# Residual additions on VectorE, four first tiles chunk by chunk, and late highs and lows spread over the down tiles, in a two-block transformer kernel

## Chip, cores and metric

One core of a Trainium2 chip runs one launch. The metric is the device time in microseconds, the median of repeated executions.

## The reference

The first block has two layers; the second adds gated deltanet, differential attention and a routed mixture of experts. The change lies in the first block and at the seam to the second. Cut to what matters:

```python
def rms_norm(x, gain):
    return x * rsqrt(mean(x * x, -1) + EPS) * gain

def hybrid_layer(x, ...):                       # twice
    h = rms_norm(x, attn_pre_gain)              # norm 1
    ...                                         # h @ w_in, two attentions, gates
    x = x + rms_norm(mixed @ w_out, attn_post_gain)          # norm 2
    h = rms_norm(x, ffn_pre_gain)                            # norm 3
    x = x + rms_norm(conv_ffn(h, w_up, conv, w_down), ffn_post_gain)   # norm 4
    return x
```

512 tokens, 1024 channels, 2816 hidden channels in each half of w_up, all float32. Behind the second layer the deltanet's input projection reads x directly.

## The kernel before

Activations lie channels by tokens: 8 chunks of 128 channels by 512 tokens. A float32 product is made of three rounded ones: each operand is split into a high part (a rounded copy, made by ScalarE) and a low part (the difference, made by VectorE), and `product` (L729 to L733) issues high × high (L731), high weight × low activation (L732) and low weight × high activation (L733). A tile of outputs (128 channels) is 8 chunks of such products, 24 matmuls, and reads one slot of weights.

**Weights.** SyncE streams 512 KB slots into a ring of 8 (L509), each as soon as the tile eight slots back has been used. ScalarE casts a slot to its high part into one of two buffers `highs` (`cast_weights`, L1420), which it may only do when the tile two before has been used; VectorE then splits off the low part in place in the ring (`split_weights`, L2035). Each engine works its list in program order, so a cast or a split that waits holds back all behind it. In layer 0 `fm` are the first tiles, then compression, token-major, gate, branch, `out`, 44 `up` and 22 `down` tiles.

**Norms.** Squares are made by ScalarE, added up by VectorE into `total`, and summed over the partitions by a matmul with ones (L788 to L798); ScalarE makes the reciprocal root `rs` (L1460, L1463). Norms 1 and 3 scale behind the products: their tiles are multiplied by `rs` when VectorE evicts them (L2165 in fm, L2296 in up), so the products can begin before `rs` is there. Norms 2 and 4 scale first: `residual_and_lows` (L2058) lets VectorE make the scaled chunk (L2063), GpSimd adds it to x (L582, function `added`), ScalarE makes the high of the sum (L1453, L1690) and its square (L1455), and VectorE the low (L2055, L2343), three chunks behind the scaling. While this runs, TensorE does a few products that nobody reads (`idle_products`, L766).

**First tiles behind a norm.** `first_pair` goes through two tiles at once, chunk by chunk: it waits for the low of chunk k, then issues the 6 products of that chunk. Its two weight highs lie in `first_high`, a part of tmp. Tiles 2 and on follow one by one (`tile`, L735); the norm's sum goes in front of tile 3; tile r uses PSUM bank r % 4 and waits, from tile 4 on, for the eviction of tile r − 4.

**Up and down.** Per up tile VectorE evicts (L2296), does a three-tap convolution (L2306, L2310), splits one coming slot, and once in two tiles multiplies (`finish`, L2285). The eviction of tile r + 1 stands in front of the convolution of tile r. ScalarE does the casts and gelu (L1614). For the down tiles the 22 chunks of the result are split into highs (`high_g`, L1619) and lows (`low_g`, L2290): 7 of them during up, 8 in one block behind it (the highs ahead of the cast of the third down tile, the lows ahead of its split), the rest one per down tile. Down tile 0 needs the eviction of the last up tile before it touches bank 0.

**Other places.** `cmp` products of the two compression blocks (L836) use banks 1 and 2 and wait for the evictions of fm tiles 9 and 10. The deltanet tiles use L1714 for eviction on ScalarE and a four-tap convolution on VectorE (L2431, L2434); behind their first pair come the a/b products (L1014), and then small decay terms (L1698 to L1703, L2391).

## Time and profile before

| | us |
|---|---|
| median of 3 runs | 3549.63 (3541.72 to 3550.85) |
| the profiled execution, its span | 3550.9 |

```profile
span 3550.9 us, 50016 instructions
## 1 busy us (share of the span) xinstructions
PE 3408.3 (96%) x16710; PEld 2674.1 (75%) x16710; DVE 2485.3 (70%) x3707; ACT 1888.2 (53%) x2964; POOL 379.1 (11%) x371
```

These are busy time, share of the span and number of instructions of each engine: PE is TensorE's matmuls, PEld its weight loads, DVE VectorE, ACT ScalarE, POOL GpSimd, SP SyncE. A busy TensorE is not one at its peak: the clock that it was granted, and matmuls that nobody reads, are not seen in this share. The chain of work that ended last, by engine:

```profile
PE 87%; DVE 6%; ACT 3%; issue 2%; DMA 1%; POOL 0%; ACTq 0%; SPq 0%; POOLq 0%; DVEq 0%
```

A timeline row is start, duration, engine, line, instruction, what it writes and reads, and in brackets the idle time of its engine before it and what ended that. Rows with a count merge instructions that follow each other, and their duration is that of all of them. Durations of single rows overlap: the next instruction of an engine starts a little before the last one's recorded end.

### The profile page before, as it was taken

How to read it: one execution, taken by the hardware profiler on the slowest of the kernel's cores; microseconds unless marked ns; L12 is line 12 of the kernel's file. 1: busy time of each engine (PE TensorE's matmuls, PEld its weight loads, DVE VectorE, ACT ScalarE, POOL GpSimd, SP SyncE). 2: the span in 40 equal slices, each digit the busy share in tenths (PEclk: the TensorE clock that was granted, in tenths of full speed). 3: DMA queues.
4: the chain of work that ended last, by engine and by line, in shares of the span. 5: the costliest groups of instructions: out<-in, count | busy, mean ns of one | idle time of the engine just before them, and what ended most of it. 6: DMA issues, size and time to landing. Idle time of an engine off the chain costs nothing.

```text
span 3550.9 us, 50016 instructions
## 1 busy us (share of the span) xinstructions
PE 3408.3 (96%) x16710; PEld 2674.1 (75%) x16710; DVE 2485.3 (70%) x3707; ACT 1888.2 (53%) x2964; POOL 379.1 (11%) x371
## 2 busy tenths in 40 slices
PE   8999999999999999999989998999999999999997
PEld 6766788787766788787778876888888676778885
DVE  6676577727677577726656547999999556579996
ACT  5666422325566422324542335888888446268885
POOL 0010100001010100001034201111111000011110
PEclk9999999999999999999999998999999999899999
DMA  4211232232211222222200007999999321189995
GB/s 163 78 43 51 75 101 95 89 100 77 78 43 54 77 95 95 92 97 86 83 30 1 7 18 260 358 364 368 358 372 386 122 72 35 42 296 371 388 382 199
DMA packets 161082, 541.88 MB, mean 153 GB/s; under 512 B 28192, under 2 KB 28192, under 8 KB 160800
## 3 DMA queue, kind: packets, MB, share of 16 engines
q1 hardware_dynamic: 141408, 510.37, 40.0%
q0 software_dynamic: 16256, 16.84, 1.4%
q10 hardware_dynamic: 3264, 12.58, 0.9%
q8 instruction: 100, 1.64, 0.2%
q14 instruction: 54, 0.44, 0.0%
HBM read 547.02 MB, written 34.60 MB: 164 GB/s over the span
## 4 chain that ended last, share of the span: by engine, by line
PE 87%; DVE 6%; ACT 3%; issue 2%; DMA 1%; POOL 0%; ACTq 0%; SPq 0%; POOLq 0%; DVEq 0%
PE psum L731 24%; PE psum L733 23%; PE psum L732 23%; PE psum L1031 4%; PE psum L881 2%; PE psum L913 2%; PE psum L895 1%; PE psum L1222 1%; DVE arena L2063 1%; PE psum L805 1%; PE psum L1228 1%; DMA arena<-rows_out_m 1%; PE psum L1171 1%; DVE arena L2391 1%; ACT highs L1420 1%
## 5 line engine op out<-in xcount | busy, mean ns | idle before, releaser
L2742 DVE TENSOR_TENSOR ew_r<-arena,ehigh_r 128x1024 fp32r<-128x1024 f32 x648 | 750.5, 1219 | 25.6 <-ACT ehigh_r L1887 25.2
L1420 ACT ACTIVATE highs<-ring 128x1024 fp32r<-128x1024 f32 x292 | 308.4, 1057 | 683.7 <-PE psum L733 677.9
L1887 ACT ACTIVATE ehigh_r<-arena 128x1024 fp32r<-128x1024 f32 x648 | 632.3, 1053 | 37.1 <-DVE arena L2733 24.0
L2035 DVE TENSOR_TENSOR ring_rounded<-ring,highs 128x1024 fp32r<-128x1024 f32 x292 | 358.4, 1228 | 417.6 <-ACT highs L1420 417.5
L733 PE MATMUL psum<-oab_r,ring_rounded 128*128 128x512 f32 x1424 | 563.8, 396 | 0.0
L731 PE MATMUL psum<-oab_r,highs 128*128 128x512 f32 x1360 | 558.6, 411 | 5.1 <-DVE fm_r L2255 4.3
L732 PE MATMUL psum<-h_r,highs 128*128 128x512 f32 x1232 | 484.3, 393 | 0.0
L731 PE MATMUL psum<-ehigh_r,xT_high_r 128*128 128x512 f32 x864 | 352.9, 408 | 12.9 <-issue 6.6
L733 PE MATMUL psum<-ehigh_r,xT_low_r 128*128 128x512 f32 x864 | 341.2, 395 | 0.0
L732 PE MATMUL psum<-ew_r,xT_high_r 128*128 128x512 f32 x864 | 339.6, 393 | 0.0
L731 PEld LDWEIGHTS psum<-oab_r,highs 128*128 128x128 f32 x1360 | 256.2, 188 | 92.1 <-issue 33.4
L733 PEld LDWEIGHTS psum<-oab_r,ring_rounded 128*128 128x128 f32 x1424 | 268.8, 189 | 59.0
L732 PEld LDWEIGHTS psum<-h_r,highs 128*128 128x128 f32 x1232 | 232.1, 188 | 44.4 <-issue 1.0
L731 PEld LDWEIGHTS psum<-ehigh_r,xT_high_r 128*128 128x128 f32 x864 | 164.3, 190 | 45.9 <-issue 15.3
L733 PEld LDWEIGHTS psum<-ehigh_r,xT_low_r 128*128 128x128 f32 x864 | 163.9, 190 | 38.5
L732 PEld LDWEIGHTS psum<-ew_r,xT_high_r 128*128 128x128 f32 x864 | 164.6, 191 | 31.9
L731 PE MATMUL psum<-ehigh_r,hT_high_r 128*128 128x512 f32 x432 | 170.4, 394 | 4.4 <-DVE hT_low_r L2755 4.4
L1031 PE MATMUL psum<-arena 128*128 128x128 f32 x1216 | 156.4, 279 | 14.8 <-issue 5.1
L733 PE MATMUL psum<-ehigh_r,hT_low_r 128*128 128x512 f32 x432 | 169.3, 392 | 0.0
L1031 PEld LDWEIGHTS psum<-arena 128*128 128x128 f32 x1216 | 146.8, 193 | 28.9 <-issue 16.8
L732 PE MATMUL psum<-ew_r,hT_high_r 128*128 128x512 f32 x432 | 167.6, 388 | 0.0
L582 POOL TENSOR_TENSOR x<-x,arena 128x512 f32<-128x512 f32 x32 | 52.6, 1670 | 938.4 <-DVE arena L2063 938.4
(383 smaller groups left out, 6249.4 us busy)
## 6 DMA issues: line engine op xcount, KB each, us to landing
arena<-in_moe_w SPq DMA_DIRECT2D x648, 512.0 KB, 5.9
ring<-in_wstream SPq DMA_DIRECT2D x312, 512.0 KB, 3.4
arena<-rows_out_m ACTq DMA_DIRECT2D x8, 1024.0 KB, 8.1
rows_in_m<-arena ACTq DMA_DIRECT2D x4, 1024.0 KB, 4.0
x<-in_xT SPq DMA_DIRECT2D x8, 256.0 KB, 7.2
result<-x SPq DMA_DIRECT2D x8, 256.0 KB, 2.1
const<-in_const SPq DMA_DIRECT2D x1, 1112.5 KB, 9.6
arena<-rows_in_m,arena POOLq DMA_INDIRECT x58, 6.4
```

Of the source, the lines that this page charges most:

```text
L582: pool.tensor_tensor(x[:, k, :], x[:, k, :], src[:, k, :], ALU.add) \
L731: pe.matmul(acc, lhs[0], rhs[0], start=start, stop=False)
L732: pe.matmul(acc, lhs[0], rhs[1], start=False, stop=False)
L733: return pe.matmul(acc, lhs[1], rhs[0], start=False, stop=stop)
L805: mm = pe.matmul(psum[:, bank, :], ones, src[:, k, :], start=(i == 0), stop=(i == KD - 1))
L881: pe.matmul(psum[:, 2 * (p % 2) + g, 0:width(p)], q[:, qt * P:(qt + 1) * P], keys, start=True, stop=True).then_inc(pe_done, seq.step(f"h{p ...
L913: mm = pe.matmul(acc, values[:, KEYS[kind], kts[i], dims], ptbuf[:, u, i * P:(i + 1) * P], start=first and i == 0, stop=last and i == n - 1)
L1031: mm = pe.matmul(psum[:, bank, c], lhsT[:, c], rhs[:, c], start=True, stop=True)
L1420: act.activation(highs[:, r % HIGHS, :], ring[:, r, :], ACT.Copy) \
L1887: act.activation(ehigh_r[p], ew[:, p, :], ACT.Copy).then_inc(expert_cast[mi], 1)
L2035: dve.tensor_tensor(ring_r[:, c % R, :], ring[:, c % R, :], high.bitcast(F32), ALU.subtract).then_inc(weights_split, seq.step(ch="split"))
L2742: TT(ew_r[p], ew[:, p, :], ehigh_r[p].bitcast(F32), ALU.subtract).then_inc(expert_split[mi], 1)
```

## The change

- GpSimd's `added` is gone. `residual_and_lows` adds each chunk to x on VectorE, right behind its scaling (and behind the low of two chunks before); norm 4's chunks 0 to 3 are first copied out of PSUM.
- `first_four` replaces `first_pair` behind norm 4 and norm 2 (fm of layer 1, up, deltanet); layer 0's first stage keeps `first_pair`. It goes through four tiles chunk by chunk: behind the high of chunk k come 8 products, behind its low 4 more. Four weight highs lie in tmp and in fm or siga. ScalarE and VectorE cast and split four tiles and a fifth ahead of the norm's scaling.
- Tile 4 gets a bank of its own and holds the norm's sum matmul in its middle. From tile 5 on the banks go (r − 5) % 4, and tile r waits for the eviction of the tile that had its bank. In fm the column products of `rs` come behind tile 4.
- In up, fm of layer 1 and deltanet the split of tile 5 stands before the stage, and the first split within it, that of tile 6, behind the work on tile 2 (deltanet: 4).
- The sums of norms 2 and 4 take one more square through VectorE and one fewer through TensorE; there are fewer idle products.
- The last up tile is evicted ahead of the split behind the convolution of tile 41. The 15 late highs and lows are spread: two behind each of the first four down tiles' casts and splits, then one each.
- The compression blocks wait for fm tiles 10 and 11.

```diff
+        LATE_HIGHS = {k: [] for k in range(PAIRS)}
+        for n in range(EARLY, PAIRS):
+            LATE_HIGHS[(n - EARLY) // 2 if n < EARLY + 8 else n - EARLY - 4].append(n)
+        first_high = two_highs("first_high", tmp[:, 0:4])
+        up_high = first_high + two_highs("up_high", fm[:, 0:4])
+        next_high = first_high + two_highs("next_high", siga[:, 4:8])
+        def bank_of_tile(r):
+            return r if r < 5 else (r - 5) % 4
-                    added("n2", y)
-                    added("n4", h)
...
+            def scaled_tile(stage, r, between=None):
+                if r >= 5:
+                    pe.wait_ge(dve_done, seq.at(f"{stage}.d{bank_before(r)}"))
+                w = [v.rearrange("p (k c) -> p k c", c=P) for v in weights()]
+                for k in range(KD):
+                    if k == KD // 2 and between:
+                        between()
+                    mm = product(psum[:, bank_of_tile(r), :], [v[:, k, :] for v in w], both_parts(k), k == 0, k == KD - 1)
+                mm.then_inc(slot_used, seq.step(f"{stage}.t{r}", ch="slot"))
+            def first_four(lows, stage, parts, high):
...
+                for k in range(KD):
+                    x_high, x_low = parts(k)
+                    pe.wait_ge(act_done, seq.at(f"{lows}.hi{k}"))
+                    for i in range(4):
+                        pe.matmul(psum[:, i, :], w[i][0][:, k, :], x_high, start=(k == 0), stop=False)
+                        pe.matmul(psum[:, i, :], w[i][1][:, k, :], x_high, start=False, stop=False)
+                    pe.wait_ge(dve_done, seq.at(f"{lows}.lo{k}"))
+                    for i in range(4):
+                        mm = pe.matmul(psum[:, i, :], w[i][0][:, k, :], x_low, start=False, stop=(k == KD - 1))
...
+                    first_four("n1", "fm", both_parts, next_high)
+                    scaled_tile("fm", 4, lambda: added_sums("n1", total))
...
-                    pe.wait_ge(dve_done, seq.at(f"fm.d{9 + kv}"))
+                    pe.wait_ge(dve_done, seq.at(f"fm.d{10 + kv}"))
...
-                sums_in_parts("n2", total, oab8, (6, 7))
-                idle_products(7, 5)
-                first_pair("n3", "up", both_parts)
+                sums_in_parts("n2", total, oab8, (7,))
+                idle_products(3, 5)
+                first_four("n3", "up", both_parts, up_high)
+                scaled_tile("up", 4, lambda: added_sums("n3", total))
...
-                sums_in_parts("n4", total, sq, (4, 5, 6))
+                sums_in_parts("n4", total, sq, (5, 6))
-                idle_products(4, 7)
+                idle_products(3, 7)
...
-            first_pair("xdn", "dn", lambda k: [xh[:, k, :], xl[k]])
+            first_four("xdn", "dn", lambda k: [xh[:, k, :], xl[k]], next_high)
...
-                for k in range(EARLY, EARLY + 8):
-                    high_g(k)
                 for k in range(PAIRS):
                     if k + HIGHS < PAIRS:
                         cast_weights()
+                    for n in LATE_HIGHS[k]:
+                        if n >= EARLY + 8:
+                            act.wait_ge(slot_used, seq.at(f"down.t{n - EARLY - 8}"))
+                        high_g(n)
...
-                first_weights()
-                cast_weights(2 + passed)
+                first_weights(next_high)
+                cast_weights(4 + passed)
                 for c in (7, 0, 1, 2, 3, 4, 5, 6):
...
-                for k in range(KD + 3):
+                for k in range(KD + 2):
                     if k < KD:
                         dve.scalar_tensor_tensor(dst[:, k, :], src(k), gain[:, k:k + 1], rs, ALU.mult, ALU.mult) \
                             .then_inc(dve_done, seq.step(f"{stage}.t{k}"))
-                    if k >= 3:
-                        low_k(k - 3)
+                    if k >= 2:
+                        low_k(k - 2)
+                    if k < KD:
+                        dve.wait_ge(dve_done, seq.at(f"{stage}.t{k}"))
+                        dve.tensor_tensor(x[:, k, :], x[:, k, :], dst[:, k, :], ALU.add) \
+                            .then_inc(dve_done, seq.step(f"{stage}.x{k}"))
...
-                    if 1 <= r <= NFM - 3:
+                    if (1 if l == 0 else 2) <= r <= NFM - 3:
                         split_weights(1)
...
-                    if r + 1 < 2 * PAIRS:
+                    if r + 1 < 2 * PAIRS - 1:
                         up_out(r + 1)
...
-                    if 1 <= r <= 2 * PAIRS - 3:
+                    if r == 2 * PAIRS - 3:
+                        up_out(2 * PAIRS - 1)
+                    if 2 <= r <= 2 * PAIRS - 3:
                         split_weights(1)
...
-                split_weights(2, of=first_high)
+                split_weights(4, of=next_high)
+                split_weights(1)
                 dve.wait_ge(pe_done, seq.at("down.c7"))
                 dve.tensor_copy(h[:, 7, :], psum[:, 7, :]).then_inc(dve_done, seq.step("down.d7"))
-                sum_of_squares("n4", sq, (7, 0, 1, 2, 3))
+                sum_of_squares("n4", sq, (7, 0, 1, 2, 3, 4))
+                for c in range(4):
+                    dve.tensor_copy(h[:, c, :], psum[:, c, :]).then_inc(dve_done, seq.step(f"down.d{c}"))
```

## Rows read from the trace of the kernel before

**Rows 1.** TensorE waits, whole span: us in total, times, longest us.
```profile
PE psum L731 <- DVE h_r L2055: 25.9, 13, 13.8
...
PE psum L731 <- DVE ring_rounded L2035: 5.3, 2, 2.7
...
PE psum L731 <- DVE arena L2296: 1.8, 2, 0.9
```

**Rows 2.** Timeline, norm 2, layer 0: start us, us, instruction, [idle before].
```profile
422.82 4.76 DVE L2063 SCALAR_TENSOR_TENSOR arena<-arena,small 128x512 f32<-128x512 f32 x4 [5.05 <-ACT arena L1463]
...
429.41 0.47 PE L731 MATMUL psum<-oab_r,first_high 128*128 128x512 f32 x1 [1.99 <-DVE h_r L2055]
...
431.54 1.76 DVE L2063 SCALAR_TENSOR_TENSOR arena<-arena,small 128x512 f32<-128x512 f32 x1
...
450.25 1.02 PE L798 MATMUL psum<-arena,const 128*128 128x512 f32 x2
...
452.02 0.63 ACT L1463 ACTIVATE arena<-arena 128x512 f32<-128x512 f32 x1
```

**Rows 3.** Timeline, VectorE: chained additions; lows; scalings read from PSUM (layer 0).
```profile
443.54 4.67 DVE L2078 TENSOR_TENSOR arena<-arena 128x512 f32<-128x512 f32 x6
...
686.46 4.90 DVE L2290 TENSOR_TENSOR g_r<-arena,oab_r 128x512 fp32r<-128x512 f32 x8
...
811.05 2.73 DVE L2063 SCALAR_TENSOR_TENSOR arena<-psum,small,arena 128x512 f32<-128x512 f32 x4 [4.62 <-ACT arena L1463]
```

**Rows 4.** Timeline, VectorE in the up tiles of layer 0.
```profile
454.77 1.28 DVE L2296 TENSOR_TENSOR arena<-psum,arena 128x512 f32<-128x512 f32 x2
...
464.40 1.22 DVE L2035 TENSOR_TENSOR ring_rounded<-ring,highs 128x1024 fp32r<-128x1024 f32 x1
```

**Rows 5.** Windows around the start of the down tiles, layers 0 and 1.
```profile
core 0: us, PE busy (x) PEld busy (x) DVE busy (x) ACT busy (x) POOL busy (x), PEclk, DMA share, GB/s
680.00:700.00 20.00, 16.44 (x58) 12.58 (x57) 14.68 (x23) 9.13 (x14) 0.00 (x0) 0.83 0.19 61
1480.00:1500.00 20.00, 16.44 (x71) 12.79 (x70) 16.11 (x24) 10.71 (x16) 0.00 (x0) 1.00 0.23 79
```

**Rows 6.** Timeline, norm 1 to fm in layer 1, TensorE, VectorE and ScalarE.
```profile
815.08 0.47 PE L731 MATMUL psum<-oab_r,first_high 128*128 128x512 f32 x1 [0.97 <-DVE h_r L2055]
...
839.51 0.68 DVE L2165 TENSOR_TENSOR arena<-psum,arena 128x512 f32<-128x512 f32 x1
...
847.02 0.69 DVE L2165 TENSOR_TENSOR arena<-psum,arena 128x512 f32<-128x512 f32 x1
...
848.35 1.06 ACT L1420 ACTIVATE highs<-ring 128x1024 fp32r<-128x1024 f32 x1 [5.53 <-PE psum L733]
...
853.87 1.06 ACT L1420 ACTIVATE highs<-ring 128x1024 fp32r<-128x1024 f32 x1 [1.84 <-PE psum L733]
```

**Rows 7.** Timeline, end of the down tiles of layer 1.
```profile
1601.05 1.06 ACT L1420 ACTIVATE highs<-ring 128x1024 fp32r<-128x1024 f32 x1 [2.56 <-PE psum L733]
...
1601.68 0.69 DVE L2333 COPY arena<-psum 128x512 f32<-128x512 f32 x1 [1.56 <-PE psum L733]
```

**Rows 8.** SyncE's ring loads from 1590 to 1630 us.
```profile
DMA to landing us min/median/max: 3.2/3.4/4.0
```

**Rows 9.** Timeline, first deltanet tiles.
```profile
1629.72 9.79 PE L1014 MATMUL psum<-small,x 128*128 128x16 f32 x64
...
1644.91 0.18 DVE L2391 TENSOR_SCALAR arena<-arena 128x32 f32<-128x32 f32 x1
...
1648.65 2.33 DVE L2434 SCALAR_TENSOR_TENSOR arena<-arena,small 128x512 f32<-128x512 f32 x3
...
1664.58 0.60 ACT L1714 ACTIVATE arena<-psum 128x512 f32<-128x512 f32 x1 [3.95 <-PE psum L733]
```

**Rows 10.** Timeline, compression products and the evictions of the last fm tiles, layer 0.
```profile
90.44 7.25 PE L836 MATMUL psum<-arena,ring 128*128 128x62 f32 x64
...
94.98 0.69 DVE L2165 TENSOR_TENSOR arena<-psum,arena 128x512 f32<-128x512 f32 x1
```

More of the change, by code:

```diff
@@ L576, in _ @@
             seq.note("zeroed")
-            def added(stage, src):
-                for k in range(KD):
-                    pool.wait_ge(dve_done, seq.at(f"{stage}.t{k}"))
-                    pool.tensor_tensor(x[:, k, :], x[:, k, :], src[:, k, :], ALU.add) \
-                        .then_inc(pool_done, seq.step(f"{stage}.x{k}"))
             for l in range(LAYERS):
@@ L789, in sums_in_parts @@
                 pe.wait_ge(dve_done, seq.at(f"{stage}.acc"))
-                pe.matmul(psum[:, bank, :], ones, acc, start=False, stop=False)
+                pe.matmul(psum[:, bank, :], ones, acc, start=(len(apart) == 1), stop=False)
                 pe.wait_ge(act_done, seq.at(f"{stage}.sq{apart[-1]}"))
@@ L1016, in _ @@
             mm.then_inc(pe_done, seq.step("ab.t"))
-            for n in range(2, 24):
+            for n in range(4, 24):
                 for k in range(KD):
@@ L2321, in _ @@
                 seq.note("down.g")
-                for k in range(EARLY, EARLY + 8):
-                    low_g(k)
                 for k in range(PAIRS):
```

112 lines of the change are left out of this document (65 added, 47 removed).

## Prediction, made before the changed kernel was run

> **What bounds the kernel now.** The page's header and its chain of waits come first: TensorE is busy for most of the span and the chain runs through its products, so time is only to be had where TensorE has nothing to do or works slowly. Next the waits of TensorE: by far the largest is that of the first products behind a norm for the low halves h_r, 25.9 us over 13 waits; the two places where a down tile waits for its split weights cost 5.3, and those where it waits for the last eviction of the up stage, 1.8 [rows 1]. These are the three things the change touches. Last, the timelines at the four norms show what makes a chunk late. In norm 2 the scaled chunks start at 422.82, the first product at 429.41, almost 7 us later [rows 2]. The scaling is four instructions in 4.76, and one later takes 1.76 beside a GpSimd addition; the same instruction fed from PSUM needs 2.73 for four [rows 2, 3]. A chunk's way is scaling, GpSimd addition, high, low; with 1.76 for the scaling and 0.6 for the low VectorE gives one in 2.4 us, while two tiles can use one in 6 × 0.23 = 1.38.
>
> A product is 0.23 us: a tile of 24 takes 853.87 − 848.35 = 5.52 [rows 6]. A signal from a tile's last product comes some 0.3 behind the time at which TensorE could issue the next.
>
> The Trainium skill (SBUF — State Buffer, Who interferes with whom) says that a VectorE instruction with two SBUF inputs and a GpSimd one that reads SBUF exclude each other for their whole length. By that rule the slow 1.76 goes when the additions leave GpSimd; the trace agrees, and its rows alone carry the prices below.
>
> **Norm 2 to up, both layers.** Removed: GpSimd's 8 additions, one sum matmul ahead of the reciprocal root (L798's kind, 1.02, of which I take 0.85), some idle products, which nothing waits for. Added on VectorE: per chunk one addition. Prices on VectorE alone: a chained addition 4.67/6 = 0.78, a low 4.90/8 = 0.61, a scaling 0.68 [rows 3]. One chunk is then 0.7 + 0.7 + 0.6 = 2.0 us, under the 4 × 3 × 0.23 = 2.76 that four tiles use. So TensorE paces the stretch, with no wait inside it.
>
> Start of scaling: 422.82 − 0.85 = 422.0. First high: scaling 0.74, addition 0.78, a ScalarE pass of 0.63 (L1463, same shape [rows 2]), 0.15 for signals: first product at 424.3 instead of 429.41. It needs only the high; the low of chunk 0 comes about 0.1 after the eight high products, taken as 0.1. Four tiles end at 424.3 + 22.1 + 0.1 = 446.5. Tile 4 holds the sum matmul in its middle (449.3) and ends, with 0.6 for it, at 452.6. From the sum matmul to rs it is 452.02 + 0.63 − 450.25 = 2.4 [rows 2], so rs stands at 451.7 and tile 0 is evicted at 452.4: tile 5 starts on time and ends at 458.2.
>
> Then the new wait. Tile 6 needs its split, which VectorE now issues only after the conv of tile 2, since the split of tile 5 has been moved ahead. Before, from the first eviction to the end of the split behind conv 3 tiles on it was 464.40 + 1.22 − 454.77 = 10.85 [rows 4], with one split (1.15) in between that is gone: 9.7. Ready at 451.7 + 9.7 = 461.4, a stall of 3.2 us. (ScalarE isn't later: its cast follows the end of tile 4 and one gelu.) Before, tile 6 started at 450.25 + 0.6 + 3 × 5.52 = 467.4. Net gain 6.0 per layer, **12.0** in all; bounds per layer are 9.2 (no stall) and 4.5 (a chunk at the 2.76 edge, first product 1.5 later). Splits after that are due at most every 5 us and the stall is not repeated.
>
> **Clock.** The windows of the down starts have the same TensorE work and the same 2.65 us stall in them, and the clock falls to its lower level in the one (0.83 over 20 us, 3.4 us of full-rate time lost) and not in the other (1.00) [rows 5]. The new stall of 3.2 is longer, so I expect the lower of the two levels (1.2 against 2.4 GHz) behind it more often than not: 0 to 3.4 per layer, 2.4 taken: **−4.8**.
>
> **Down start, both layers.** The last up tile is evicted ahead of a split, not behind it, so the 0.9 goes. Eight highs and eight lows in a block stood ahead of the cast and split of down tile 2; now that cast follows tile 0, two highs and lows follow it, and the others go two, then one, behind each next tile. Tile 2's split waits only for the last two finishes (about 1 us before TensorE needs it), tile 3's is done 2 to 3 us early. Highs 7 to 14 are needed five tiles (27 us) later; they are hidden. Gain 5.3 + 1.8 = **7.1** [rows 1], and the clock fall of layer 0, **3.2** (bounds 0 to 3.4) [rows 5]. If the cover fails it is a split and two lows, 2.4, per layer.
>
> **Norm 4 to fm, layer 1.** ScalarE now casts five tiles, and VectorE splits four and one, ahead of the copy of bank 7 that starts the squares. The fifth cast waits for the end of down tile 20, as the cast at 1601.05 does in layer 1; cast 1.06 and split 1.22 put the copy of layer 1 at 1603.3 instead of 1601.68 [rows 4, 7], and that of layer 0 1.6 later likewise. One sum matmul less takes 0.85 off and one more addition puts some back: scaling starts about 1.3 later. The way to the first product was 815.08 − 811.05 = 4.0 [rows 3, 6] and is 2.3: first product at 814.7. Four tiles to 836.9, tile 4 with its sum to 843.0, the four column products about 1.2, tile 5 to 849.7. rs is at 836.9 + 2.76 + 2.4 = 842.1. The split of tile 6 follows two evictions with their blocks, a third eviction and itself: 847.02 − 839.51 − 1.25 + 0.6 + 1.2 = 8.1 [rows 6], ready at 850.2, a stall of 0.5. Before, tile 6 started at 853.6. Gain **3.4**. Layer 0's first stage is fed by loads as before; its evictions only change banks: 0.
>
> **Norm 4 to deltanet.** Here the fifth cast is also queued behind a transfer. Ring slots are refilled eight tiles on, and with the two padding slots the fifth tile's slot is the one that down tile 20 frees, at about 1601. It lands 3.4 later [rows 8], so ScalarE's squares and VectorE's copy, both queued behind that cast and split, wait too: copy at 1601.1 + 3.4 + 1.1 + 1.2 = 1606.9, 5.2 later than 1601.68, scaling 4.5 later, first product 4.5 − 1.7 = 2.8 later. TensorE has no work for over 5 us there. The pair before ended at 1629.5. How long it took is read in layer 1's fm, worked back from tile 4's signal through three tiles, the sum and the columns: 848.35 − 0.3 − 3 × 5.52 − 0.6 − 1.2 − 815.08 = 14.6 [rows 6]. So the four end at 1629.5 − 14.6 + 2.8 + 22.2 = 1639.9. The a/b products follow; from them to the end of VectorE's decay terms it is 15.4 [rows 9], then convs 2, 3 and 4 (2.33 + 0.47 each) and the split of tile 6: 25.1 behind the four, 1665.0. Before, tile 6 started at 1664.3. Loss 0.7, in which 1.3 is a stall for that split; the clock's fall in the empty stretch costs 1 to 4, 2.5 taken: **−3.2**. Bound the other way: the slot is there in time, +2.3.
>
> **Compression.** Its second block of products now waits for tile 11's eviction, 94.98 + 0.69 = 95.7, and could have begun at 90.44 + 7.25/2 = 94.1 [rows 10]. Behind it a wait for ScalarE takes some of that: 0 to 1.6 per layer, 0.9 taken, **−1.8**.
>
> **Sum.** 12.0 − 4.8 + 7.1 + 3.2 + 3.4 − 3.2 − 1.8 = 15.9 us. Off the profiled 3550.9 this is 3535.0; the median of the runs, 3549.6, is 1.3 lower, which gives 3533.7, **3534**.
>
> **Rivals.**
> The stalls are hidden: the clock stays up behind them and the slot arrives in time. 4.8 + 2.5 + some of the 6.5 of stalls back: about 3525. For it: layer 1's 2.65 without a fall; against: the longer pause.
> The clock falls more: at every pause of 2 us or more, norm 4 of layer 0 among them, and for the full length. 1.0 more at each tile 6, 2 at norm 4, 1.5 at deltanet, 2 to 3 on the way: 3543. For it: the rows at the lower level; against: the pauses at norm 4 are broken by sum matmuls.
> The change doesn't do what it says: the five casts and splits delay the scaling in norm 2 as in norm 4, 4 us per layer: 3542. Against: there they begin two tiles before the end of the out stage.
> Slower: VectorE's two-input scalings and lows keep the 1.76 with GpSimd idle. A chunk is 1.76 + 1.76 + 0.78 = 4.3, 1.5 over 2.76; over 8 chunks and 4 norms 49 us less the 15.9: about 3582. It decides from a chunk of 3.25 on (15.9/32 over 2.76). Against: 0.61 for a low [rows 3].
> The chunk is slow for another reason: VectorE pauses behind every instruction. With a pause of half an instruction's length a chunk is 1.5 × (0.74 + 0.74 + 0.69) = 3.3, 0.5 over: 17 us, 3551. The eight lows in 4.90 leave no such gap [rows 3]. The Trainium skill (VectorE: DVE Perf Modes, The DRAIN you can't avoid) has such a pause as a rule, the instruction's length less 266 ns; by it a chunk would be about 3.5 and the time, an estimate, 3555; the trace does not bear it out here.
>
> **Chances.** Forecast 0.54, hidden stalls 0.18, more clock falls 0.18, late casts 0.05, slow VectorE 0.03, pauses 0.02. The forecast's own range is 3528 to 3541. The range of 8 in 10 takes in the first rivals' centres: 3524 to 3544. A measurement of this kernel tells 0.3% (10.7 us, 3539) from no change. Faster: 0.18 and nine tenths of 0.54, 0.67. Slower 0.03, same 0.30.
>
> **What would show it.** Right: no wait for h_r over 0.5 us inside the four tiles; about 22 us from first high product to their end; a wait for ring_rounded of some 3.2 at tile 6 of up in each layer and 0.5 at fm; no wait for ring_rounded at down tile 2; an empty TensorE of over 5 us at the end of layer 1 behind a cast that waits for a load. Wrong: chunks arriving slower than 2.76, a low over 0.8, or a stall at a down tile further on.

## The result, and the profile after

| | before | after |
|---|---|---|
| median | 3546.83 us (3540.22 to 3553.04, 20 runs) | 3540.10 us (3534.15 to 3542.81, 20 runs) |
| the profiled execution, its span | 3550.9 | 3532.3 |

The ratio is 0.9981, with a 95% interval of 0.9974 to 0.9987: the change gains 6.7 us, a small gain, but the interval leaves out no change at all. The forecast was a gain of 15.9 and a time of 3534; the time lies in the range of 3524 to 3544, but the gain is under half of what was forecast and within the 0.3% that was called no change, to which 0.30 was given, where 0.67 was given to faster.

The two profiled executions differ by 18.6 us, far more than the medians do. The one of after is the fastest of its 20. The part behind 1713.63 us of before, in which no line is changed, took 3550.9 − 1713.63 = 1837.3 us, and 3532.3 − 1702.99 = 1829.3 in after, with a granted clock of 0.98 against 0.97. These 8.0 us are no gain of the change, and the comparison by stages below stops ahead of them.

The page of after, in its header:

```profile
## 1 busy us (share of the span) xinstructions
PE 3392.3 (96%) x16682; PEld 2669.3 (76%) x16682; DVE 2488.3 (70%) x3751; ACT 1887.1 (53%) x2964; POOL 326.6 (9%) x339
```

GpSimd has lost its 32 additions and VectorE has gained them. VectorE's busy time is hardly more, since its scalings no longer run beside GpSimd. The waits of TensorE in the first 1760 us of after (us in total, times, longest):

```profile
PE psum L737 <- DVE h_r L2098: 13.0, 1, 13.0
PE psum L737 <- DVE ring_rounded L2078: 9.4, 4, 3.2
PE psum L825 <- ACT arena L1694: 5.8, 2, 4.4
...
PE psum L877 <- DVE arena L2213: 3.2, 2, 1.6
```

Of the 13 waits for h_r [rows 1] the first of the program is left. The waits for ring_rounded now stand elsewhere than in before: two at tile 6 of up, one at tile 6 of the deltanet and a small one at fm. The wait of L825 (the first sum matmul of norm 4, for the squares) and that of L877 (the second block of the compression, for the eviction of tile 11) are new. The last evictions of up, waited for at L731 in before, are not among them.

**Norm 2.** VectorE, ScalarE and TensorE behind the reciprocal root of layer 0, where before had [rows 2]:

```profile
425.00 0.75 DVE L2106 SCALAR_TENSOR_TENSOR arena<-arena,small 128x512 f32<-128x512 f32 x1 [3.16 <-ACT arena L1503]
425.78 0.69 DVE L2112 TENSOR_TENSOR x<-x,arena 128x512 f32<-128x512 f32 x1
...
426.51 0.72 ACT L1493 ACTIVATE oab_r<-x,small 128x512 fp32r<-128x512 f32 x1 [0.60 <-DVE x L2112]
...
427.37 0.47 PE L777 MATMUL psum<-oab_r,first_high 128*128 128x512 f32 x1 [1.22 <-ACT oab_r L1493]
...
429.70 0.74 DVE L2106 SCALAR_TENSOR_TENSOR arena<-arena,small 128x512 f32<-128x512 f32 x1
430.37 0.74 DVE L2098 SCALAR_TENSOR_TENSOR h_r<-x,small,oab_r 128x512 fp32r<-128x512 f32 x1
431.03 0.68 DVE L2112 TENSOR_TENSOR x<-x,arena 128x512 f32<-128x512 f32 x1
431.63 0.74 DVE L2106 SCALAR_TENSOR_TENSOR arena<-arena,small 128x512 f32<-128x512 f32 x1
...
463.53 1.22 DVE L2078 TENSOR_TENSOR ring_rounded<-ring,highs 128x1024 fp32r<-128x1024 f32 x1
...
464.89 0.47 PE L737 MATMUL psum<-oab_r,highs 128*128 128x512 f32 x1 [2.98 <-DVE ring_rounded L2078]
```

The first product comes 2.4 us behind the first scaling, where before needed 6.6 [rows 2], and a chunk takes 431.63 − 429.70 = 1.93 on VectorE. Tile 6 waits 2.98 for its split.

**By stages.** The scalings behind the norms and the first products of the compression are good marks. Those of before that are not in the rows ahead of the prediction are these, and the last is a deltanet tile behind which nothing differs:

```profile
892.26 1.00 PE L836 MATMUL psum<-arena,ring 128*128 128x62 f32 x8
...
1225.95 1.42 DVE L2063 SCALAR_TENSOR_TENSOR arena<-arena,small 128x512 f32<-128x512 f32 x2 [5.06 <-ACT arena L1463]
...
1611.32 1.41 DVE L2063 SCALAR_TENSOR_TENSOR arena<-psum,small,arena 128x512 f32<-128x512 f32 x2 [4.62 <-ACT arena L1463]
...
1713.63 0.47 PE L731 MATMUL psum<-x_part,highs 128*128 128x512 f32 x1 [1.07 <-ACT arena L1714]
```

and those of after:

```profile
89.37 3.68 PE L877 MATMUL psum<-arena,ring 128*128 128x62 f32 x32
...
804.34 0.75 DVE L2106 SCALAR_TENSOR_TENSOR arena<-arena,small 128x512 f32<-128x512 f32 x1 [1.13 <-ACT arena L1503]
...
881.47 1.22 PE L877 MATMUL psum<-arena,ring 128*128 128x62 f32 x10
...
1217.23 0.75 DVE L2106 SCALAR_TENSOR_TENSOR arena<-arena,small 128x512 f32<-128x512 f32 x1 [3.18 <-ACT arena L1503]
...
1600.73 0.75 DVE L2106 SCALAR_TENSOR_TENSOR arena<-arena,small 128x512 f32<-128x512 f32 x1 [2.28 <-ACT arena L1503]
...
1702.99 0.47 PE L737 MATMUL psum<-x_part,highs 128*128 128x512 f32 x1 [1.08 <-ACT arena L1757]
```

The forecast column puts the terms of the prediction into the stage where they fall (norm 2 to up: 0.85 of the 6.0 ahead of the scaling, 5.15 behind it; the late scalings of norm 4, 1.3 and 4.5, behind the down tiles).

| stage (us) | before | after | change | forecast |
|---|---|---|---|---|
| start to compression, layer 0 | 90.44 [rows 10] | 89.37 | −1.1 | 0 |
| to the scaling of norm 2, layer 0 [rows 2] | 332.4 | 335.6 | +3.2 | +0.05 |
| to the scaling of norm 4, layer 0 [rows 3] | 388.2 | 379.3 | −8.9 | −8.2 |
| to the compression, layer 1 | 81.2 | 77.1 | −4.1 | −4.7 |
| to norm 2, layer 1 | 333.7 | 335.8 | +2.1 | +0.05 |
| to norm 4, layer 1 | 385.4 | 383.5 | −1.9 | −1.8 |
| to the deltanet tile | 102.3 | 102.3 | −0.05 | −1.3 |
| sum | 1713.6 | 1703.0 | −10.7 | −15.9 |

Five of the seven come within about 1.3 us of their forecast. The two that don't are the stretches with the compression: 3.2 and 2.0 us too slow, 5.2 together, which is all of the difference between 15.9 and 10.7.

**Compression.** The timeline of its products in after, layer 0 (before: 64 products in 7.25 [rows 10]):

```profile
94.65 5.36 PE L877 MATMUL psum<-arena,ring 128*128 128x62 f32 x32 [1.61 <-DVE arena L2213]
...
100.26 0.54 PE L738 MATMUL psum<-ring_rounded,oab_r 128*128 128x408 f32 x1
100.60 0.54 PE L739 MATMUL psum<-highs,h_r 128*128 128x408 f32 x1
```

The wait of 1.6 us is the one that was predicted. What was not predicted is behind it: the second 32 products take 5.36 us where the first took 3.68, and the products behind it have a pitch of 0.34, where at the full clock it is 0.18 to 0.19 (shown with the idle products below). That is the lower level of the clock (1.2 GHz), and the windows of the two kernels say so (columns as in [rows 5]):

```profile
80.00:100.00 20.00, 18.39 (x107) 16.51 (x106) 15.71 (x23) 14.47 (x23) 0.00 (x0) 0.91 0.46 154
100.00:120.00 20.00, 20.00 (x106) 19.10 (x106) 7.48 (x16) 8.32 (x19) 0.00 (x0) 0.91 0.32 106
```

These two rows are from after. In before the window of 100 to 120 us has 1.00, and so has this one:

```profile
80.00:100.00 20.00, 20.00 (x125) 18.04 (x124) 15.66 (x22) 14.49 (x22) 0.00 (x0) 1.00 0.51 163
```

Twice 0.09 of 20 us is 3.6 us of full-rate time lost (the same work would have taken that much less at the higher level). This gave the theory for the experiments: **the change does what was forecast, and the compression's short wait, by the clock that falls behind it, takes back most of what is missing.** The rivals: the norms part never gained what the rows suggested; the other new waits (tile 6, norm 4) carry the miss; the gain of the down start is smaller than forecast.

### The profile page after: what moved, and what is told of

It is laid out like the page before. It is cut to its first block, busy times and chain, and to the rows that moved or that the text cites. A ratio compares the mean times of both kernels' runs of the same rounds, so it can differ in the third digit from the quotient of the medians.

```text
span 3532.3 us, 49964 instructions
## 1 busy us (share of the span) xinstructions
PE 3392.3 (96%) x16682; PEld 2669.3 (76%) x16682; DVE 2488.3 (70%) x3751; ACT 1887.1 (53%) x2964; POOL 326.6 (9%) x339
## 4 chain that ended last, share of the span: by engine, by line
PE 88%; DVE 5%; ACT 4%; issue 1%; DMA 1%; POOL 0%; ACTq 0%; SPq 0%; POOLq 0%; DVEq 0%
PE psum L737 23%; PE psum L739 22%; PE psum L738 22%; PE psum L1071 4%; PE psum L922 2%; PE psum L954 2%; PE psum L936 1%; PE psum L1262 1%; PE psum L777 1%; PE psum L778 1%; PE psum L781 1%; PE psum L842 1%; DVE ring_rounded L2078 1%; PE psum L1268 1%; DMA arena<-rows_out_m 1%
## 5 line engine op out<-in xcount | busy, mean ns | idle before, releaser
L1460 ACT ACTIVATE highs<-ring 128x1024 fp32r<-128x1024 f32 x284 | 300.1, 1057 | 650.1 <-PE psum L739 640.3
L2078 DVE TENSOR_TENSOR ring_rounded<-ring,highs 128x1024 fp32r<-128x1024 f32 x284 | 348.8, 1228 | 398.4 <-ACT highs L1460 398.3
L737 PE MATMUL psum<-oab_r,highs 128*128 128x512 f32 x1312 | 540.7, 412 | 11.3 <-DVE ring_rounded L2078 6.2
L739 PE MATMUL psum<-oab_r,ring_rounded 128*128 128x512 f32 x1328 | 526.7, 397 | 0.0
L738 PE MATMUL psum<-h_r,highs 128*128 128x512 f32 x1184 | 467.1, 395 | 0.0
L737 PEld LDWEIGHTS psum<-oab_r,highs 128*128 128x128 f32 x1312 | 247.7, 189 | 97.4 <-issue 40.9
L739 PEld LDWEIGHTS psum<-oab_r,ring_rounded 128*128 128x128 f32 x1328 | 251.3, 189 | 55.0
L738 PEld LDWEIGHTS psum<-h_r,highs 128*128 128x128 f32 x1184 | 224.0, 189 | 42.2 <-issue 1.0
L597 POOL TENSOR_TENSOR arena<-arena 128x512 f32<-128x512 f32 x32 | 40.9, 1279 | 1076.9 <-ACT arena L1610 1076.9
```

The lines of the kernel that those rows point to most:

```text
L597: pool.tensor_tensor(big[:, n * T:(n + 1) * T], big[:, n * T:(n + 1) * T], rs, ALU.mult) \
L737: pe.matmul(acc, lhs[0], rhs[0], start=start, stop=False)
L738: pe.matmul(acc, lhs[0], rhs[1], start=False, stop=False)
L739: return pe.matmul(acc, lhs[1], rhs[0], start=False, stop=stop)
L1460: act.activation(highs[:, r % HIGHS, :], ring[:, r, :], ACT.Copy) \
L2078: dve.tensor_tensor(ring_r[:, c % R, :], ring[:, c % R, :], high.bitcast(F32), ALU.subtract).then_inc(weights_split, seq.step(ch="split"))
```

## Experiments

All are measured in the same way as the pair above, beside runs of the kernel before on the same chip, which had medians of 3548.3, 3547.0 and 3548.4 in the three groups of runs. Differences below are worked out from the ratios (0.001 is 3.5 us), and an interval of a ratio is 2 to 5 us to either side, so that of a difference of two kernels 4 to 7. The kernel after was not run again in these groups; it is compared through before, whose medians lie within 1.6 us of each other. Each kernel was profiled once, and its stages are read from that one execution.

| kernel | median | ratio to before | to after |
|---|---|---|---|
| after | 3540.1 | 0.9981 (0.9974 to 0.9987) | |
| down part alone | 3533.5 | 0.9959 (0.9946 to 0.9972) | −7.8 |
| norms part alone | 3550.9 | 1.0007 (0.9998 to 1.0016) | +9.2 |
| norms part, no wait in the compression | 3542.5 | 0.9982 (0.9973 to 0.9991) | +0.4 |
| after, no wait in the compression | 3528.7 | 0.9948 (0.9933 to 0.9963) | −11.7 |
| after, idle products over that wait | 3533.7 | 0.9971 (0.9960 to 0.9982) | −3.5 |
| after, all up splits earlier | 3548.4 | 1.0003 (0.9992 to 1.0014) | +7.8 |
| after, only tile 6's split earlier | 3530.8 | 0.9957 (0.9943 to 0.9970) | −8.5 |
| after, fifth cast behind the squares | 3531.8 | 0.9954 (0.9940 to 0.9969) | −9.6 |
| after, additions on GpSimd again | 3548.1 | 1.0006 (0.9996 to 1.0016) | +8.9 |
| all mends together | 3517.5 | 0.9921 (0.9908 to 0.9935) | −21.3 |

**The two parts by themselves.** The kernel before, with the changes at the start of the down tiles and nothing else:

```
+        LATE_HIGHS = {k: [] for k in range(PAIRS)}
...
+                    if r == 2 * PAIRS - 3:
+                        up_out(2 * PAIRS - 1)
                     if 1 <= r <= 2 * PAIRS - 3:
                         split_weights(1)
...
                     if k + HIGHS < PAIRS:
                         split_weights(1)
-                    if k + EARLY + 8 < PAIRS:
-                        low_g(k + EARLY + 8)
+                    for n in LATE_HIGHS[k]:
+                        low_g(n)
```

> The kernel before with one part of the change alone: the late highs and lows spread over the down tiles and the last up tile evicted ahead of a split; the norms, the additions on GpSimd and the first pairs stay. Forecast's step: the two waits at the down start, 2.65 and 0.9 in each layer, are gone, 7.1 us, and the clock fall behind the longer one, which only some executions have, 0 to 6.8 more: 7 to 11 us under the kernel before. Rival A (the down start carries the whole measured gain, the norms give nothing): the same 7, and then the whole change is no better than this. Rival B (the spread highs and lows make a later down tile wait): under 3 us gained, and a wait for ring_rounded or a low further on in the down tiles.

It is 3533.5 us, 14.5 under before by the ratio, with 10.3 forecast for this part (7.1 and 3.2). The forecast is inside the interval of 10 to 19, at its small end. By the profiled executions, from the scaling of norm 2 to that of norm 4, it is 381.1 us in both layers against 388.2 and 385.4 in before: 7.1 and 4.3, together 11.3. Unlike in the profiled execution of before, this kernel has no stretch at the lower clock between 350 and 900 us. The complement, the changed kernel with these edits taken back:

> The change without its down-projection part: the norms (residual additions on VectorE, first four tiles chunk by chunk, split and cast places, the freed slots) as in the kernel after, the late highs and lows and the last eviction at the start of the down projection as in the kernel before. The down part alone had the ratio 0.9959, and the whole change 0.9981, so by subtraction the norms part alone should lose about 8 us: my theory gives 1.0010 to 1.0035. The rival, that parts do not add because the down part's gain is luck of the clock, gives 0.998 here as well. The forecast's own sum for this part, 12.0 + 3.4 - 3.2 - 4.8 - 1.8 = 5.6 us of gain, would be 0.9984.

The norms part alone is 2.5 us slower than before (0.7 faster to 5.7 slower; 3.5 to 12 slower was expected), where its terms in the forecast sum to a gain of 5.6. The parts add up to a gain of 12 and the whole gains 6.7; with intervals of this size the difference is not told from none. So the miss of the prediction lies in the norms part, about 8 us of it.

**The compression without its wait.** In after, the blocks use banks 1 and 2, of which bank 2 is freed last but one; here they use banks 0 and 1, each free in time.

```
-                    pe.wait_ge(dve_done, seq.at(f"fm.d{10 + kv}"))
+                    pe.wait_ge(dve_done, seq.at(f"fm.d{9 + kv}"))
...
-                            mm = pe.matmul(psum[:, 1 + kv, 0:2 * NC], w[:, i, :],
+                            mm = pe.matmul(psum[:, kv, 0:2 * NC], w[:, i, :],
...
                     pe.wait_ge(act_done, seq.at("cmp.hid1"))
+                    pe.wait_ge(dve_done, seq.at("fm.d11"))
```

> The changed kernel, but the compression blocks collect in banks 0 and 1 and wait for fm tiles 9 and 10, as before the change, and not for tile 11. Theory W (the 1.6 us wait in the middle of the small products also brings the clock down, which costs as much again): 3.5 us per layer, 7 us under the changed kernel, no low clock at the compression stage. Rival (the forecast's own term, the wait less what the next wait takes back): 1.8 us under the changed kernel. Rival 2: the wait moves to the products behind it for ScalarE's outputs and nothing is gained, within 1 us.

The time falls by 11.7 us against after (about 6 to 17), 5.8 per layer, for a wait of 1.6; 7 was expected. Its products are as in before again, and the clock stays up:

```profile
90.04 7.25 PE L877 MATMUL psum<-arena,ring 128*128 128x62 f32 x64
...
80.00:100.00 20.00, 20.00 (x125) 18.14 (x124) 16.01 (x22) 14.47 (x23) 0.00 (x0) 1.00 0.57 171
```

The same edit on the norms part alone:

> As the kernel with the norms part alone, with the compression's blocks in the two banks that are free earliest, so that neither block waits. If the wait of 1.6 us in the compression and the clock that falls behind it are what the forecast sized too small, this is 8 to 12 us below the kernel with the norms part alone: 0.9975 to 1.000. The rival, that the norms part loses somewhere else (tile 6, norm 4), leaves the two within 4 us of each other.

8.9 us by the ratios, from 1.0007 to 0.9982, with 8 to 12 expected. With the wait gone the norms part gains 6.4 us, where the forecast without its compression term has 7.4. The rival that the norms part never had its gain is gone.

**The wait or the clock.** After, with two idle products (each a high and a low pass, into a bank that nobody reads) ahead of the second block's wait:

```
                 for kv in range(2):
+                    if kv:
+                        idle_products(2, 7)
                     pe.wait_ge(dve_done, seq.at(f"fm.d{10 + kv}"))
```

> The kernel after, with two idle products (into a bank that nobody reads) ahead of the second compression block's wait; nothing else is changed, and the block still waits for the same eviction. It separates the wait from the clock. My theory is that the wait itself costs only its 1.6 us per layer and that the clock that falls behind it (6.8 us at half speed in the profiled execution, over 10 us in another) costs the rest: with TensorE busy over the wait the clock stays up, the stretch from the compression's start to the first weighing product goes from 38.9 us to about 36 us per layer, and the time falls by 5 to 9 us against the kernel after, to a ratio of 0.9955 to 0.9968 against the kernel before. The rival, that the wait for the bank costs the time whatever the clock does, gives the ratio of the kernel after, 0.998, or slightly more for the idle products.

The timeline of the same stretch:

```profile
92.92 1.94 PE L803 MATMUL psum<-const 128*128 128x512 f32 x4
94.69 3.78 PE L879 MATMUL psum<-arena,ring 128*128 128x62 f32 x32
...
98.55 0.35 PE L738 MATMUL psum<-ring_rounded,oab_r 128*128 128x408 f32 x1
98.74 0.34 PE L739 MATMUL psum<-highs,h_r 128*128 128x408 f32 x1
```

The second block starts no earlier than in after (94.69 against 94.65), but takes 3.78 in place of 5.36, and the window of 80 to 120 us has the clock at 1.00. From the compression's start to the first weighing product it is 125.06 − 89.40 (the start of the first block) = 35.7, against 128.25 − 89.37 = 38.9 in after and 34.8 without the wait: of the 4.1 us that the wait costs in this profiled execution 0.9 is the wait itself, as forecast, and 3.2 is the clock. In the time of the whole kernel the idle products bring 3.5 us by the ratio (6.4 by the medians), less than the 5 to 9 that was expected, and the kernel without the wait is another 8 faster. By the medians alone the share of the clock stays open.

The other traces narrow it down. This is the stage from the compression's first product to the first scaling of norm 2 (the second and fifth rows of the table by stages), in the profiled executions of the changed kernel and of those made from it with the norms part in, in us:

| kernels | layer 0 | layer 1 |
|---|---|---|
| with the wait: after, norms alone, up splits, tile 6, fifth cast, additions back | 335.6, 337.3, 335.8, 339.8, 337.3, 335.8 | 335.8, 337.4, 337.4, 335.8, 337.2, 337.4 |
| without it: after, norms alone, all mends | 331.6, 331.5, 333.0 | 332.9, 331.8, 332.9 |
| idle products over it | 332.6 | 332.4 |

The means are 336.9, 332.3 and 332.5. The wait with all that follows costs 4.6 us per layer, 9.2 in both, and the idle products give back 4.4 of the 4.6, though the second block starts no earlier. So nearly all of the price is the clock, and 0.2 to 0.9 us per layer the wait itself. Up to the scaling of norm 4 in layer 1 the two kernels are equally fast too (1594.20 with idle products, 1594.61 without the wait): the 8 us between their ratios don't stem from this stage in their profiled executions.

A longer fall than that of the profiled execution is common: the profiled run of the kernel with the fifth cast moved, in which nothing of the compression is changed, has 0.87 in place of 0.91 in this window, and in that of 100 to 120 too: 5.2 us lost in place of 3.6. Over the six kernels with the wait and both layers, the fall behind it lasted 6.8 us five times and 10.2 us seven times; in after it was 6.8 in both. The first of the two windows of the kernel with the fifth cast moved:

```profile
80.00:100.00 20.00, 18.39 (x104) 16.64 (x102) 15.70 (x24) 14.49 (x22) 0.00 (x0) 0.87 0.41 142
```

So the profiled execution of after, the fastest of its 20, was lucky here too, and the 5.2 us of the stage table are the low end of what the compression costs; the 9.2 of the stages and the 11.7 and 8.9 us of the two runs without the wait are the better price.

**Tile 6 of up.** First with every split moved ahead by two tiles, and every cast by one:

```
-                    if 2 <= r <= 2 * PAIRS - 3:
+                    if r <= 2 * PAIRS - 5:
                         split_weights(1)
```

> The changed kernel, but in up VectorE splits tile r+6 behind the convolution of tile r from r = 0 on (not from r = 2 on for tile r+4), and ScalarE casts it one step earlier, ahead of the first gelu. Theory: the wait of 2.98 us at up tile 6 is gone in both layers and with it the clock fall of 3.4 us behind it (1.6 each): 6 to 9 us under the changed kernel. Rival (the wait only moves on to tile 7, whose cast stands behind the end of tile 5): under 2 us gained, a wait for ring_rounded at tile 7.

This missed: 7.8 us slower than after, where 6 to 9 faster was expected. The wait at tile 6 goes, but all later splits now stand in VectorE's queue ahead of evictions, where they wait for casts that ScalarE makes only when TensorE has freed a slot. At the end of the stage the last eviction has come so late that the first down product waits for it:

```profile
680.52 0.80 PE L737 MATMUL psum<-spare_r,highs 128*128 128x512 f32 x1 [6.17 <-DVE arena L2347]
```

A split that is early for TensorE is late for what is queued behind it. In each layer the wait of 2.98 became one of 6.17, with the clock down behind it. So only tile 6's split and its cast were moved, and the others left:

```
-                    if r >= 4:
+                    if r == 3 or r >= 5:
                         cast_weights()
...
-                    if 2 <= r <= 2 * PAIRS - 3:
+                    if r == 0 or 3 <= r <= 2 * PAIRS - 3:
                         split_weights(1)
```

> The kernel after, with the up projection's tile 6 alone split earlier (at the first eviction in place of the third) and its cast put ahead of the first gelu; all later tiles keep their places. My theory: the 2.98 us wait at tile 6 and the half-speed stretch of 3.4 us behind it (1.7 us lost) are both on the path, in each layer, so 2 x (2.98 + 1.7) = 9.4 us are to be had, less what the earlier split delays: a ratio of 0.9955 to 0.9965 against the kernel before. The rival: the wait only moves to another tile or to the start of the down projection, as it did when all splits were moved; then the ratio stays at 0.998 and a wait of 2 us or more stands elsewhere between 425 and 690 us.

8.5 us of the 9.4 are there (by the stage from norm 2 to norm 4 in the profiled executions 3.3 and 3.5, 6.8 together). The wait is 1.23 now, at tile 7, and the window behind it has its clock at 1.00, which is 0.91 in after:

```profile
473.20 0.47 PE L737 MATMUL psum<-oab_r,highs 128*128 128x512 f32 x1 [1.23 <-DVE ring_rounded L2078]
...
460.00:480.00 20.00, 18.77 (x82) 14.99 (x82) 19.57 (x29) 6.64 (x7) 0.00 (x0) 1.00 0.30 103
```

**The fifth cast.** After, with ScalarE's fifth cast behind the squares of norm 4, and VectorE's split of it behind the lows:

```
                 first_weights(next_high)
-                cast_weights(4 + passed)
...
                         .then_inc(act_done, seq.step(f"n4.sq{c}"))
+                cast_weights(4 + passed)
```

> The changed kernel, but behind the down tiles the fifth cast follows the squares of norm 4, and its split the norm's lows. Theory: in layer 1 the squares no longer wait for the transfer, so TensorE's pause of 4.4 us ahead of the sums shrinks to about 0.5 and the clock stays up, and in layer 0 1.3 us come back: 5 to 8 us under the changed kernel. Rival (the cast now delays the reciprocal root, or the split the first eviction): 2 us or less.

This is 9.6 us faster than after, where 5 to 8 was expected. In after the cast waits 3.95 us for a load, and squares and copy are queued behind it; TensorE is empty for 4.42 us:

```profile
1588.02 1.06 ACT L1460 ACTIVATE highs<-ring 128x1024 fp32r<-128x1024 f32 x1 [3.95 <-DMA ring<-in_wstream]
...
1594.58 1.66 PE L825 MATMUL psum<-arena,const 128*128 128x512 f32 x2 [4.42 <-ACT arena L1694]
```

and here the same sum matmul waits 0.16 and takes 1.12:

```profile
1591.44 1.12 PE L825 MATMUL psum<-arena,const 128*128 128x512 f32 x2 [0.16 <-ACT arena L1693]
```

The forecast had 1.3 and 4.5 us for the later scalings and 2.5 for the clock, 8.3 together. So the two other new waits, at tile 6 (8.5 us for 9.4) and at norm 4 (9.6 for 8.3), cost about what was forecast, and the rival that they carry the miss is gone too.

**The additions.** After with the additions on GpSimd again and the lows three chunks behind; the order of the products stays:

```
                 for k in range(KD + 3):
...
-                    if k < KD:
-                        dve.wait_ge(dve_done, seq.at(f"{stage}.t{k}"))
-                        dve.tensor_tensor(x[:, k, :], x[:, k, :], dst[:, k, :], ALU.add) \
-                            .then_inc(dve_done, seq.step(f"{stage}.x{k}"))
+                    if k >= 3:
+                        low_k(k - 3)
```

> The kernel after with one part undone: the residual additions of both norms run on GpSimd again, and the lows trail them by three chunks in place of two; the order of the first four tiles, the compression and the down projection stay as in the kernel after. My theory: what releases the first product behind a norm is then a chunk later and VectorE is slowed beside GpSimd's additions, 0.7 to 3 us for each of the four norms, so 3 to 12 us more than the kernel after: a ratio of 0.999 to 1.0015. The rival: VectorE's own additions cost as much as GpSimd's neighbourhood did, nothing changes and the ratio stays at 0.998.

8.9 us slower than after, 2.2 for each of the four norms. The timeline of norm 2:

```profile
425.47 4.77 DVE L2115 SCALAR_TENSOR_TENSOR arena<-arena,small 128x512 f32<-128x512 f32 x4 [3.18 <-ACT arena L1512]
426.30 6.78 POOL L597 TENSOR_TENSOR x<-x,arena 128x512 f32<-128x512 f32 x4 [94.69 <-DVE arena L2115]
428.03 0.72 ACT L1502 ACTIVATE oab_r<-x,small 128x512 fp32r<-128x512 f32 x1 [1.65 <-POOL x L597]
...
431.85 1.77 DVE L2115 SCALAR_TENSOR_TENSOR arena<-arena,small 128x512 f32<-128x512 f32 x1
```

ScalarE starts the first high 428.03 − 425.47 = 2.6 us behind the first scaling, against 1.5 in after, and the two engines hold each other up: 1.70 for an addition, 1.77 for a scaling beside one, where a scaling in after takes 0.74. This is the rule of the Trainium skill that the prediction drew on (SBUF — State Buffer, Who interferes with whom), and the trace agrees. So with the new order of products the move of the additions, with the lows that follow them one chunk sooner, is worth 8.9 us. The order of the products apart from them was not tried.

**All together.** The banks of the compression, tile 6's split, the fifth cast, and the split that feeds tile 6 of the deltanet ahead of the convolution of tile 4 and not behind it (what was expected calls it the down projection; the edit is in the deltanet):

```
                 dve.wait_ge(act_done, seq.at(f"dn.d{n}"))
+                if n == 4:
+                    split_weights(1)
...
-                if n >= 4:
+                if n >= 5:
                     split_weights(1)
```

> The kernel after with four mends together: the compression's blocks in the banks that are free earliest, so that neither waits; tile 6 of the up projection split earlier; the fifth cast behind the squares of norm 4 and its split behind the lows; the split that feeds tile 6 of the down projection made earlier. My theory is that the change's chunk order is worth what was forecast once these four waits and the clock that falls behind them are gone: the compression gave -11.7 us alone, the fifth cast -9.6 us alone, tile 6 should give -9, and half of that is likely to overlap or to be spent in another fall of the clock, so 3515 to 3524 us, a ratio of 0.991 to 0.9935 against the kernel before. The rival: the gains of the single mends are mostly the same clock luck counted twice, and the sum is no better than the best single one, 0.9948.

3517.5 us, a ratio of 0.9921: 28 us under before, 21 under after. The single mends sum to 11.7 + 8.5 + 9.6 = 29.8 and, with the fourth, give 21.3 together, 8.5 less than their sum; with intervals of this size that is not told from none, and that the same clock was counted twice is a guess. Between 1230 and 1700 us no wait of TensorE over 1.3 us is left, and the windows of 80 to 120, 460 to 480 and 1580 to 1600 us have the clock at 1.00; behind that, from 1600 to 1620, it still falls, to 0.72. This kernel beats both.

## Why the prediction was right, and where not

**Norm 2 to up**, 6.0 per layer with a stall of 3.2: right. From the scaling's start to the reciprocal root of norm 3 it was 29.7 by the forecast (451.7 − 422.0) and 30.0 in the trace; the chunk was 1.93 for 2.0, the first product 2.4 behind the scaling for 2.3, and the stall 2.98. No wait for h_r stands inside the four tiles.

**Clock behind tile 6**, 2.4 per layer: the fall is there in both layers, and 2.98 + 1.7 was a fair price for both together (8.5 us measured for the pair of layers, 9.4 expected). The fall itself was 1.7 per layer and not 2.4. What failed is the reasoning beside it: the text looked for falls of the clock behind pauses of 2 us and more alone.

**Down start**, 10.3: no wait for ring_rounded and none for the last eviction stands at the first down tiles, and the clock is at 1.00 in both layers:

```profile
677.00:697.00 20.00, 20.00 (x88) 16.32 (x87) 14.36 (x20) 8.02 (x12) 0.00 (x0) 1.00 0.33 105
1477.00:1497.00 20.00, 20.00 (x88) 16.32 (x88) 9.60 (x12) 6.92 (x10) 0.00 (x0) 1.00 0.23 79
```

(the windows that answer to [rows 5], moved with the stage). The term held or was too small: 14.5 measured for it alone, 11.3 by its stages. That it held is in part luck. The 3.2 rest on one execution of before; of six waits of 2.65 us that the profiled executions have at this place (before, and the two kernels with the norms part alone), two were followed by a lower clock, both in layer 0, for 6.8 and 3.4 us.

**Norm 4 to fm**, 3.4: right. Counted from the scaling, which was to start 1.3 later, the stage gained 4.1 for 4.7, and the stall at tile 6 of fm is 0.28 for 0.5.

**Norm 4 to deltanet**, −3.2: the queueing behind the load is as foreseen (3.95 for a landing of 3.4, an empty TensorE of 4.42 for "over 5"). The stall at tile 6 of the deltanet is 3.19 and not 1.3. The step that failed is the price of the convs, 2.33 + 0.47 each [rows 9]: in after the first of them starts together with two GpSimd instructions, which in before ran in VectorE's own pause of 3.04 us, and takes 1.38 + 2.99, which is 1.5 of the 1.9 that the stall was short by. The clock's share was too small as well: by windows of 20 us from 1580 to 1660 us after lost 8.8 us of full-rate time and before 5.2, 3.6 for the 2.5 that was taken.

```profile
1640.90 1.38 DVE L2486 TENSOR_SCALAR arena<-arena,small 128x512 f32<-128x512 f32 x1
...
1642.32 2.99 DVE L2489 SCALAR_TENSOR_TENSOR arena<-arena,small 128x512 f32<-128x512 f32 x3
...
1640.95 1.05 POOL L615 TENSOR_TENSOR arena<-const,arena 128x512 f32<-128x512 f32 x1 [517.56 <-DVE arena L2446]
```

**Compression**, −1.8: the mis-sized term, and nearly the whole error. The wait was named, placed and sized rightly (1.6), its cost of 0.9 per layer as a wait is what the run with idle products shows, and its effect on the clock was left at nothing. By the two runs without the wait it cost 8.9 and 11.7 us in all, and 9.2 by the stages, so the term was short by 7 to 10; with their mean, 10.3, in place of 1.8 the sum is a gain of 7.4, where 6.7 was measured.

**The time and the rivals.** The measured 3540.1 lies at the upper end of the forecast's own range of 3528 to 3541, and luck helped it there. The median of three runs from which the time was reckoned, 3549.6, was 2.8 above that of 20 runs, 3546.8; and the down part gave 4 us more than forecast while the norms part gave 8 less.

The time also lies between the forecast and the rival "the clock falls more" (3543), whose "2 to 3 on the way" is the only place where the text allowed for it. In kind it is that rival that came about, behind a shorter pause than it named. The hidden stalls, the late casts behind norm 2, the slow VectorE and the pauses of VectorE did not come about; the last by the pitch of 431.03 − 430.37 = 0.66 us behind an instruction of 0.74, an overlap and no pause. The section cited for it (the Trainium skill, VectorE: DVE Perf Modes, The DRAIN you can't avoid) gives the gap as a rule, but adds that a next instruction that is not held starts earlier; the trace shows the second. The 3555 of that rival is also a slip: a chunk of 3.5 is 0.74 over 2.76, 24 us over 32 chunks, and gives 3557.

**Chances.** 0.67 went to a gain above 10.7 us, on a sum of 15.9 whose every term came from one execution of a kernel whose runs differ by up to 13 us. That execution showed where the clock had fallen, not how often it does, and the short new wait was not given a share of that doubt.

## What to carry to other kernels

Price a new wait of TensorE twice: its own length, of which some is hidden, and the clock behind it, which was not hidden here. Here 1.6 us in the midst of products of 62 columns cost 4.4 to 5.8 us per layer, so a bank or a buffer that is free one tile earlier is worth more than the wait that the profile shows. Where a wait can't be avoided, idle products over it kept the clock here. And a piece moved ahead in an in-order queue has to be followed to what then stands behind it: one split moved gained 8.5 us, all of them moved lost 7.8.

## What was not expected of the hardware

The lower clock came behind a TensorE wait of 1.61 us between blocks of 32 products of 62 columns, in both layers of every profiled kernel here that had the wait uncovered (six: the changed one and five experiments), and cost 3.4 to 5.2 us of full-rate time over the 40 us of the two windows of layer 0. With the wait filled by four 512-column products, or taken away, the same two windows kept 1.00. A wait of 1.23 us between dense tiles (tiles of 512-column products without a pause) left the clock at 1.00 in all four places where two kernels had it; one of 2.98 brought a window of 20 us to about 0.91 in 13 of the 14 places of seven kernels, and not in layer 1 of the kernel with the additions on GpSimd again; one of 2.65 did so in two places of six [rows 5]. So the same wait doesn't always have the same price. The Trainium skill (TensorE: Matmul & The Clock Gate, Part 1: The HAM clock gate) names the same two levels, 1.2 and 2.4 GHz, and the trace agrees. It also warns that how much of a kernel runs at the lower level varies between executions of one kernel; each kernel here was profiled once, so the traces show such a difference only between kernels with the same wait.
